# Hybrid mixer of a two-block network: norms and a scan placed later in the heads' loop, three output tiles begun instead of two

## The reference, cut to what matters

```python
def hybrid_mixer(h, cos, sin, ...):
    proj = h @ w_in
    q_a, kv_a, k_pe, z, xbc, dt_raw = jnp.split(proj, ...)
    q = (rmsnorm_2(q_a, ...) @ w_q_up).reshape(b, s, MLA_HEADS, QK_HEAD_DIM)
    q_nope, q_pe = jnp.split(q, [QK_NOPE_DIM], axis=-1)          # 64 and 32 wide
    kv = (rmsnorm_2(kv_a, ...) @ w_kv_up).reshape(...)
    k_nope, v = jnp.split(kv, [QK_NOPE_DIM], axis=-1)
    q_nope = rmsnorm_2(q_nope, ...)
    q_pe = rope(rmsnorm_2(q_pe, ...), cos, sin)
    k_nope = rmsnorm_2(k_nope, ...)
    ...
    attn_out = causal_attention(q_full, k_full, v)
    xbc = silu(causal_depthwise_conv(xbc) + conv_b)
    dt = jax.nn.softplus(dt_raw + dt_bias)
    y = ssd_chunked(xs, dt, a, bm, cm) + d_skip * xs             # cumsum of dt * a per chunk
    yg = rmsnorm_2(y * jax.nn.silu(z), ...) * ssd_norm_w
    return jnp.concatenate([attn_out, yg], axis=-1) @ w_out
x = x + g1 * hybrid_mixer(...)
```

## Time and profile before

| | |
|---|---|
| median of 3 runs | 3398.59 us (3398.4 to 3402.43) |
| profiled execution | 3401.71 us, its span 3400.0 us |
| PE busy | 3320.0 us, 98% of the span |
| PEld, DVE, ACT, POOL busy | 2743.0, 1781.8, 1157.1, 68.3 us |
| mean granted TensorE clock | 0.981 of full speed |
| hybrid mixer's loop and end, layer 0 | about 2213 to 2360 us of the span |
| the same, layer 1 | about 2847 to 2992 us |

### The profile page before, as it was taken

One profiled execution on the slowest core, in us unless ns is written; L12 is line 12 of the kernel. 1 busy time (PEld: TensorE's weight loads), 2 busy tenths in 40 slices (PEclk: granted clock), 3 DMA queues, 4 the chain that ended last, 5 costly groups with the idle time before them and its releaser, 6 DMA issues.

```text
span 3400.0 us, 37008 instructions
## 1 busy us (share of the span) xinstructions
PE 3320.0 (98%) x15359; PEld 2743.0 (81%) x15359; DVE 1781.8 (52%) x2517; ACT 1157.1 (34%) x1598; POOL 68.3 (2%) x96
## 2 busy tenths in 40 slices
PE   7999999999999999999999999999999999999999
PEld 6888876888888888887788887877788888878887
DVE  5664365666446664364666545775433347553332
ACT  4322253322233222362322223553322235432221
POOL 1000000000000000000000001100000010000000
PEclk9999999999999999999999999999999999999999
DMA  5443321444333443321244432211222322023322
GB/s 150 139 148 115 106 75 62 129 144 142 110 115 112 137 137 126 96 80 57 75 149 137 132 115 83 84 38 38 81 93 96 103 73 79 9 75 99 97 95 68
DMA packets 334141, 339.85 MB, mean 100 GB/s; under 512 B 12182, under 2 KB 329048, under 8 KB 333976
## 3 DMA queue, kind: packets, MB, share of 16 engines
q1 hardware_dynamic: 332696, 333.98, 30.8%
q0 software_dynamic: 1280, 3.50, 0.4%
HBM read 335.36 MB, written 2.10 MB: 99 GB/s over the span
## 4 chain that ended last, share of the span: by engine, by line
PE 89%; DVE 6%; ACT 3%; issue 1%; DMA 1%; POOL 0%; SPq 0%; DVEq 0%; POOLq 0%; ACTq 0%
PE ps L135 88%; DVE ar L100 1%; ACT ar L95 1%; PE ps L138 1%; DVE ar L108 1%; DVE wl L100 1%; ACT L95 1%; ACT wh L95 1%; ACT ch L95 0%; DVE ar L117 0%; DMA raw<-in_ffn_w 0%; DMA ar<-in_ple_proj 0%; DVE ar L104 0%; DVE x L100 0%; DVE hl L108 0%
## 5 line engine op out<-in xcount | busy, mean ns | idle before, releaser
L135 PE MATMUL ps<-hh,wl 128*128 128x512 f32 x2760 | 1091.9, 396 | 21.7 <-DVE hl L108 14.8
L100 DVE TENSOR_TENSOR wl<-raw,wh 128x1024 fp32r<-128x1024 f32 (+2 forms) x547 | 655.2, 1200 | 825.0 <-ACT wh L95 824.6
L135 PE MATMUL ps<-hl,wh 128*128 128x512 f32 x2760 | 1080.8, 392 | 0.0
L135 PE MATMUL ps<-hh,wh 128*128 128x512 f32 x2760 | 1080.3, 391 | 0.0
L95 ACT ACTIVATE wh<-raw 128x1024 fp32r<-128x1024 f32 (+2 forms) x547 | 560.2, 1027 | 495.4 <-PE ps L135 480.8
L135 PEld LDWEIGHTS ps<-hh,wl 128*128 128x128 f32 x2760 | 522.5, 189 | 138.3 <-issue 30.2
L135 PEld LDWEIGHTS ps<-hh,wh 128*128 128x128 f32 x2760 | 522.2, 189 | 110.2
L135 PEld LDWEIGHTS ps<-hl,wh 128*128 128x128 f32 x2760 | 523.0, 189 | 105.7 <-issue 0.2
L135 PE MATMUL ps<-uh,wl 128*128 128x512 f32 x1056 | 411.8, 390 | 0.0
L135 PE MATMUL ps<-uh,wh 128*128 128x512 f32 x1056 | 410.9, 389 | 0.0
L135 PE MATMUL ps<-ul,wh 128*128 128x512 f32 x1056 | 410.8, 389 | 0.0
(11 more groups left out here) (213 smaller groups left out, 2710.0 us busy)
## 6 DMA issues: line engine op xcount, KB each, us to landing
raw<-in_ffn_w SPq DMA_DIRECT2D x120, 1024.0 KB, 5.3
raw<-in_w_ada SPq DMA_DIRECT2D x48, 1024.0 KB, 5.2
raw<-in_w_gate_up SPq DMA_DIRECT2D x44, 1024.0 KB, 5.0
raw<-in_m_w_in SPq DMA_DIRECT2D x26, 1024.0 KB, 5.6
raw<-in_w_down SPq DMA_DIRECT2D x16, 1024.0 KB, 5.2
raw<-in_ffn_w SPq DMA_DIRECT2D x16, 768.0 KB, 4.4
raw<-in_w_in SPq DMA_DIRECT2D x12, 1024.0 KB, 5.3
raw<-in_m_w_out SPq DMA_DIRECT2D x8, 1024.0 KB, 5.4
```

Source lines behind the costliest of these rows:

```text
L100: return self.issue(lambda e: e.tensor_tensor(out, a, b, op))
L135: return self.issue(lambda e: e.matmul(out, l, r, start=start, stop=stop, skip_group_check=True))
```

## The change

Four edits, all in the two hybrid mixers. (1) `normed` is cut in two: what it keeps is the reciprocal and the rotary part of the queries; the two wide multiplies (queries and keys without rotation, 128x1024 each) go to a new function `normed_nope`. For heads 0 to 3 both are called in a row; for heads 4 to 7 `normed(1)` moves from after xb tile 2 to after tile 3, and `normed_nope(1)` stands after tile 4. (2) The scan trio moves from after xb tile 3 to after tile 6. (3) Three output tiles are begun instead of two. (4) PE runs slices 0 and 1 of the begun tiles before the state space part ends, instead of slices 0 to 3.

```diff
@@ PE
-                rest = begin(s, [("out", 0), ("out", 1)], ch, cl, (s, "c"), (0, 1, 2, 3))
+                rest = begin(s, [("out", t) for t in range(3)], ch, cl, (s, "c"), (0, 1))
@@ ACT and DVE, each
-                begin(s, [("out", 0), ("out", 1)])
+                begin(s, [("out", t) for t in range(3)])
@@ DVE, normed
                     dve.own()
-                    dve.tt(pe, pe, r[2].to_broadcast([128, 4, 4, 32]), MUL).then_inc(worked, (s, "qpn", sd))
-                    dve.tt(nope, nope, r[1].to_broadcast([128, 4, 4, 64]), MUL).then_inc(worked, (s, "qn", sd))
-                    dve.wait_ge(worked, (s, "qpn", sd))
+                    dve.tt(pe, pe, stats(rs, sd, 2).unsqueeze(3).to_broadcast([128, 4, 4, 32]), MUL).then_inc(worked, (s, "qpn", sd))
+                    dve.own()
                     dve.wait_ge(pooled, (s, "kpe"))
...
-                    dve.wait_ge(worked, (s, "qps", sd, 1))
+                    dve.own()
                     dve.tt(pe, pe, CW, MUL).then_inc(worked, (s, "qpc", sd))
-                    dve.tt(kn, kn, r[0].to_broadcast([128, 4, 4, 64]), MUL).then_inc(worked, (s, "knorm", sd))
-                    dve.wait_ge(worked, (s, "qpc", sd))
-                    dve.tt(pe, pe, t2, ADD).then_inc(worked, (s, "qkn", sd))
+                    dve.own()
+                    dve.tt(pe, pe, t2, ADD).then_inc(worked, (s, "qpe", sd))
+
+                def normed_nope(sd):
+                    q, kn = by_head(Qt, 96, sd)[:, :, :, 0:64], by_head(Kt, 64, sd)
+                    dve.wait_ge(worked, (s, "rs", sd))
+                    dve.tt(q, q, stats(rs, sd, 1).unsqueeze(3).to_broadcast([128, 4, 4, 64]), MUL).then_inc(worked, (s, "qn", sd))
+                    dve.tt(kn, kn, stats(rs, sd, 0).unsqueeze(3).to_broadcast([128, 4, 4, 64]), MUL).then_inc(worked, (s, "qkn", sd))
...
                 normed(0)
+                normed_nope(0)
@@ DVE, between
-                    if t == 2:
+                    if t == 3:
                         normed(1)
-                    if t == 3:
+                    if t == 4:
+                        normed_nope(1)
+                    if t == 6:
                         dve.wait_ge(curved, (s, "dln"))
...
                         dve.scan(ad[32:40, :], cm[32:40, :], w8[32:40, :]).then_inc(worked, (s, "ad"))
```

More of the change, by code:

```diff
@@ L2456, in normed @@
                     dve.recip(rs[:, c], ss[:, c]).then_inc(worked, (s, "rs", sd))
-                    q = by_head(Qt, 96, sd)
-                    pe, nope, kn = q[:, :, :, 64:96], q[:, :, :, 0:64], by_head(Kt, 64, sd)
+                    pe = by_head(Qt, 96, sd)[:, :, :, 64:96]
                     t2 = A(14, 2).rearrange("p a n -> p (a n)").rearrange("p (b h n) -> p b h n", b=4, n=32)[:, :, 4 * sd:4 * sd + 4, :]
                     CW, SW = (A(38)[:, a:a + 128].rearrange(tok4, b=4).unsqueeze(2).to_broadcast([128, 4, 4, 32]) for a in (256, 384))
-                    r = [stats(rs, sd, i).unsqueeze(3) for i in range(3)]
                     dve.own()
-                    dve.tt(pe, pe, r[2].to_broadcast([128, 4, 4, 32]), MUL).then_inc(worked, (s, "qpn", sd))
-                    dve.tt(nope, nope, r[1].to_broadcast([128, 4, 4, 64]), MUL).then_inc(worked, (s, "qn", sd))
-                    dve.wait_ge(worked, (s, "qpn", sd))
+                    dve.tt(pe, pe, stats(rs, sd, 2).unsqueeze(3).to_broadcast([128, 4, 4, 32]), MUL).then_inc(worked, (s, "qpn", sd))
+                    dve.own()
                     dve.wait_ge(pooled, (s, "kpe"))
```

## The result

| | before | changed |
|---|---|---|
| median, first comparison (4 runs each) | 3399.78 us | 3418.36 us (3415.33 to 3419.39) |
| ratio, with its 95% interval | | 1.0052 [1.004, 1.0064] |
| median, measured again (10 and 5 runs) | 3400.74 us | 3416.92 us (3414.63 to 3419.64), ratio 1.0047 [1.0034, 1.0059] |
| profiled execution | 3401.71 us | 3418.11 us |
| its span, mean granted clock | 3400.0 us, 0.981 | 3416.4 us, 0.977 |

The changed kernel is slower by 16 to 19 us, 0.5%. The forecast was 3411.6 us, with a range from 3401 to 3419. DVE's busy time rose by 1.1 us and PE's by 10.7 us, though PE does the same matmuls. So 10.7 of the 16.4 us between the two spans are time in which PE was at work and slower, which points at the half clock.

The account below looks back on a forecast made before the run. PE holds 89% of the span, but DVE sets the pace just after the moved work. -0.3 (DVE order) + 5.3 (output tiles) + four clock falls at 2.0 = +13.0 us on 3398.6: 3411.6 us, range 3401 to 3419.

Parts of the forecast that it names:

- rival (d): Heads' loop: the clock stays low through `values(1)` and the scores after it, 4 to 5 us a layer; +19, 3417.6 us; 9%.
- The wait in `turn(0)` goes: Heads' loop: DVE reaches head 1's minima 3.8 us earlier, so PE's 2.81 and 2.85 us wait vanishes, 1.1 us to spare.
- the lead is not kept: Heads' loop up to `values(1)`: DVE's stretch to head 3's minima stays 44.3 to 44.5 us; worth -0.3 us over both layers.
- The three waits together: Heads' loop: PE waits in the first `turned`, the second `turned` and `values(1)`, about 6 us in all.
- The clock behind the broken-up waits: Heads' loop: half clock lasts until PE has worked again after `values(1)`; 2.0 us a layer, bounds 0 and 5.
- Part 2: Output tiles: begun tiles gain 3.0 and 2.5 us, then tile 3's late split makes PE idle 5.4 us; costs 5.3 us.
- The clock fall behind it: Output tiles: the clock falls behind PE's 5.4 us wait before tile 3, costing 2.0 us in each layer.
- (a): Heads' loops and output tiles: the clock falls in none of the four places; +5.0 us, 3403.6 us; 15%.
- (b): Heads' loop: the lead is kept and PE no longer waits at `values(1)`, -8.0 us; with output tiles +1.3 us; 10%.
- (c): Heads' loop and output tiles: the lead is kept and tile 3's split is not late; -13.5 us, 3385 us; 6%.

Follow-up runs that it names:

- small exponentials first: Changed kernel with ACT's two small exponentials of the chunk ends ahead of the Silu of xb tiles 4 to 7: 3404.32 us, ratio 1.0014 to the kernel before.
- all moves: Changed kernel with ACT's high parts before exponentials of heads 1 and 2, small exponentials before the Silu, output tile 3 split earlier: 3386.35 us, ratio 0.996 to before.
- early split: Changed kernel with output tile 3's split behind the update of x tile 0, ahead of its square: 3402.41 us, ratio 1.0011 to the kernel before.
- the two runs of one part each: Kernel before with only the DVE edits (norms, scan trio): 3407.05 us; kernel before with only the three begun output tiles, two slices first: 3410.8 us.
- ACT's splits first: Changed kernel with ACT's high parts, two xb tiles on, ahead of the exponentials of heads 1 and 2: 3405.34 us, ratio 1.0015 to the kernel before.
- the output tiles only: Kernel before with three output tiles begun, slices 0 and 1 first, DVE's order in the heads' loop unaltered: 3410.8 us, ratio 1.003.
- tiles and early split on before: Kernel before with three output tiles begun, two slices each, and tile 3's split behind the update of x tile 0: 3399.87 us, ratio 1.0001.
- all moves on before: Kernel before with three begun tiles, both ACT reorderings and tile 3's earlier split, but DVE's norms and scan unmoved: 3397.53 us, ratio 0.9992.

## Why the prediction was right, and where it was short

Slower was right, and 3418.4 lies in the range; the sum was 13.0 us, measured were 18.6 and 16.2, 16.4 by the spans of the two profiled executions. The range took in rival (d) as well as the sum, so that the time lies in it doesn't yet say that the terms were right.

- **The wait in `turn(0)` goes.** Right. The minima of head 1 come at 2225.30, and PE goes through `turn(0)` at 2227.22 without a wait.
- **But the lead is not kept.** Right to 0.1 us. The minima of head 3 were forecast 44.3 to 44.5 us after the first split and came after 44.37 in both layers; `values(1)` was forecast 9.82 us behind and came 9.82 behind (2267.18 - 2257.36; 2907.96 - 2898.14). PE waits 1.90 us there, "about 2" forecast. The three waits together were forecast at about 6 us and were 3.57 in layer 0 (1.06, 0.61, 1.90) and 2.30 in layer 1 (0.40, 1.90). What the forecast didn't have is why 9.82 is a constant: it took the number for DVE's pace, and it is ACT's queue. The exponentials of head 3, a Silu between two table loads and then two small exponentials come one behind the other, and DVE stands still for 4.57 us meanwhile. The runs with the small exponentials first (8.00 us) and with all moves (8.59) show this.
- **The clock behind the broken-up waits: the step that failed.** The forecast took 2.0 us a layer, "nearest to that of 2232.40 to 2236.20", with 0 and 5 as bounds. It measured 6.25 and 4.97 us (useless matmuls inside the wait, against the changed kernel), in layer 0 over the upper bound. It also saw one half clock that lasts up to `values(1)`, where the trace has the clock back at 1.00 from 2264 to 2266 and a second fall within the last wait. I had rated a long stretch at half clock as rival (d) at 9%, and this is what happened: 13 us at 0.50, through `values(1)`, the scores and the transposes behind it. Its place was right and its price (+19 in all) close to the median. The row I sized it by lay in dense 512-column matmuls; the row at 0.50 ahead of the output tiles, 10.10 us of small matmuls, transposes and a few of 512 columns, which had served only for the upper bound, was the nearer one, since the work behind `values(1)` is small matmuls too. Ahead of the output tiles PE took 1.6 and 1.1 us less than before (states to out). That this is the loss coming back isn't shown, since the stretch differs by as much between kernels with the same code there.
- **Part 2.** Right. Forecast: 0.8 and 1.2 us of waiting for `wl` of tile 2 (0.69 and 1.59), no waits at slices 4 to 7, 5.4 us of idle PE before tile 3 (5.17 in both layers), tile 3 late by 2.4 and 2.9 us. It starts 25.56 us after out in layer 0 (2364.96 - 2339.40), against 23.02 before (2359.52 - 2336.50): +2.5; layer 1 25.46 against 22.54, +2.9. The clock fall behind it, 2.0 forecast, came to 1.8 and 2.3 by the run with the early split, if all that is not the wait is put down to it.
- **The rivals.** (a) and (b) fall with the two runs of one part each. (c), faster by 13.5 us with the lead kept and tile 3's split in time, is wrong for this change, but with three moves added on ACT and DVE it came out at 13.7. That the numbers meet is partly luck. In the trace with all moves out to done is 2.3 us shorter than before in the two layers, where (c) had 5.5; the first split to the states is 9.5 us shorter (58.26 and 58.42 against 63.94 and 62.27), where it had 8.0; and 3.2 us lie in states to out, which (c) did not count.

Made again with the measured terms: -0.5 for DVE (44.37 against 45.47 and 43.80), +11.2 for the clock in the loops, -2.7 in states to out, +5.5 for the tiles and +4.1 for the clock behind them: +17.6 us.

The Trainium skill ("Perfetto Trace Analysis", Optimizing Scalar/DVE Operations) had spoken for rival (b): where DVE isn't saturated but makes others wait, breaking up its instructions may let work end sooner. The trace agrees in part: the minima of head 1 came 3.9 us sooner behind the first split (12.31 us against 16.24) and the wait there went, yet the time rose by 7.2 us until ACT's queue was reordered too (-11.4). By the Trainium skill ("TensorE: Matmul & The Clock Gate", Part 4: PE-mode transpose) transposes don't count for the clock as matmuls do, so that it would stay low up to `values(1)`. The trace agrees only in part. The clock was low at `values(1)`, and it was at 0.50 while PE had only transposes from 2260 to 2263, but it rose to 0.96 in the next microsecond and to 1.00 in the one after, with nothing but transposes on PE since 2257.50. In the run with useless matmuls inside the wait it rose likewise, from 0.50 at 2261 to 2262 to 0.87 in the next microsecond, ahead of those matmuls.

## What to carry to other kernels

When a wait is removed, look for the next instruction that the same chain of engines gates, and measure its distance from the last common event: here two layers with different clocks had the same 9.82 us, which says that the gain will not reach beyond it, and it pays to follow the distance through every queue in it (here to two tiny exponentials behind a table switch) before the first wait is moved. A wait that is broken into short ones next to small matmuls can cost more than the long one, by the clock: price a fall by a stretch of the same kind of work, not by the nearest one in time. And a split, a copy or a load that a later tile needs belongs in its queue ahead of the bookkeeping of the tiles before it, above all when tiles are made to end together.

## What the runs showed of the hardware that I had not expected

The clock stayed at half for 13 us in which PE was busy almost throughout (12.82 of 13 us from 2267 to 2280, granted 0.50), with matmuls of 64 to 512 columns and transposes. It fell within an idle time of 1.90 us; a shorter fall behind 1.06 us before that (0.66 from 2259 to 2264) was over by then, and an idle time of 0.61 us between them brought none. With 1.06 and 0.82 us (small exponentials first) there was only a short fall, and the clock was back before `values(1)`; with one idle time of 1.31 us (all moves) none at all; in layer 1 0.89 us (ACT's splits first) left `values(1)` at full clock too. In layer 0 of that run 0.47 and 1.90 us brought 13 us at 0.50 again, from 2260 to 2273. Seven matmuls of 512 columns, 1.6 us of useless work inside the wait, avoided it and were worth 9 to 11 us. The same idle time does not always bring a fall: behind the wait in `turn(0)` of layer 1 the clock stayed at 1.00 in the trace of before (2.85 us) and fell to 0.50 in the runs with the output tiles only (2.81), with tiles and early split on before (2.85) and with all moves on before (2.82). Nothing here shows which property of the work holds the clock down.
